# Convolution taps moved between an attention kernel's softmax steps and its first heads

## The reference

```python
h = _rmsnorm(x, g_pre_mix)
z = h @ w_in + b_in
q, k, v, cva, cvg = jnp.split(z, [D_ATTN, 2 * D_ATTN, 3 * D_ATTN, 3 * D_ATTN + D_CV], axis=-1)
attn = moba_fn(q, k, v)                       # 8 heads x 64, blocks of 256, best 3 blocks and the own one
glu = cva * jax.nn.sigmoid(cvg)
c = _causal_dwconv(jnp.concatenate([cv_hist, glu], axis=1), w_cv_dw, b_cv_dw)   # 31 taps, 512 channels
c = jax.nn.silu(_layernorm(c, g_cv_ln, b_cv_ln)) @ w_cv_pw + b_cv_pw
x = x + _rmsnorm(jnp.concatenate([attn, c], axis=-1) @ w_out, g_post_mix)
# then a gated feed-forward part with a convolution of three taps, 1024 -> 2 x 2816 -> 1024
```

## Time and profile before

| what | value |
|---|---|
| median of 3 runs | 1112.55 us (1112.46 to 1114.36) |
| the profiled execution | 1111.6 us |
| its span in the trace | 1109.8 us |
| mean granted clock of TensorE | 0.935 of 2.4 GHz |
| busy: PE, PEld | 956.3 us (86%), 702.5 us (63%) |
| busy: DVE, ACT, POOL | 697.8 us (63%), 446.0 us (40%), 460.2 us (41%) |
| moved by DMA | 205.19 MB, mean 185 GB/s |

### The profile page before, as it was taken

How to read it: one execution, slowest core, us unless ns; L and a number is a source line. 1 busy time by engine, 2 the same in 40 slices (tenths; PEclk the granted TensorE clock), 3 DMA queues, 4 the chain that set the end, 5 groups by cost and what they waited for, 6 DMA issues and landing times.

```text
span 1109.8 us, 19606 instructions
## 1 busy us (share of the span) xinstructions
PE 956.3 (86%) x7520; PEld 702.5 (63%) x7520; DVE 697.8 (63%) x920; ACT 446.0 (40%) x892; POOL 460.2 (41%) x408
## 2 busy tenths in 40 slices
PE   3987869798795088987989987999999999999995
PEld 3545655454453045544645567999999999667663
DVE  3688695867574047677442556888888889523215
ACT  3334454666666644435230223233333323234332
POOL 1014355656563943461000334654556555323430
PEclk9998988989898579989899998999999999999998
DMA  9896979998988337886958211223322231222222
GB/s 320 294 314 230 352 250 320 330 351 302 324 306 282 134 119 231 283 281 221 398 173 236 74 41 39 77 77 95 96 77 77 77 114 39 76 65 87 76 72 85
DMA packets 155207, 205.19 MB, mean 185 GB/s; under 512 B 10097, under 2 KB 75634, under 8 KB 155072
## 3 DMA queue, kind: packets, MB, share of 16 engines
q1 hardware_dynamic: 154619, 202.33, 54.8%
q10 hardware_dynamic: 495, 1.62, 0.5%
HBM read 198.59 MB, written 5.68 MB: 184 GB/s over the span
## 4 chain that ended last, share of the span: by engine, by line
PE 68%; DVE 9%; POOL 9%; ACT 6%; issue 4%; DMA 2%; SPq 2%; POOLq 0%; DVEq 0%; ACTq 0%
POOL conv L1822 7%; PE tp L880 7%; PE z L880 6%; PE sc L880 6%; PE z L740 5%; PE sc L530 5%; PE ob L590 4%; PE z L625 4%; PE ob L880 3%; PE sm L880 3%; PE tp L911 3%; PE ob L911 3%; PE z L911 2%; PE sc L706 2%; DVE kT L1422 2%
## 5 line engine op out<-in xcount | busy, mean ns | idle before, releaser
L1822 POOL TENSOR_TENSOR conv<-conv,prod 128x576 f32<-128x576 f32 x120 | 174.8, 1457 | 122.9 <-ACT prod L1095 107.8
L1422 DVE STREAM_TRANSPOSE kT<-kN 128x2048 f32<-128x2048 f32 x64 | 145.6, 2295 | 35.4 <-DMA kN<-in_cache_k 34.9
L1094 ACT ACTIVATE prod<-glu,consts 128x512 f32<-128x512 f32 x124 | 89.1, 718 | 54.0 <-POOL conv L1822 50.2
L1862 POOL TENSOR_TENSOR wulo<-wu,wuhi 128x2048 fp32r<-128x2048 f32 x22 | 102.4, 4656 | 13.1 <-ACT wuhi L1164 13.1
L1880 POOL TENSOR_TENSOR wdlo<-wd,wdhi 128x1024 fp32r<-128x1024 f32 x22 | 57.4, 2610 | 90.0 <-ACT wdhi L1353 90.0
L1729 DVE TENSOR_TENSOR fTlo<-fT,fThi 128x1152 fp32r<-128x1152 f32 x22 | 29.7, 1355 | 91.6 <-ACT fThi L1352 91.6
L625 PE MATMUL z<-hT,wz 128*128 128x512 f32 x192 | 85.4, 598 | 0.0
L530 PE MATMUL sc<-kT,qS 128*32 128x256 f32 x1024 | 68.1, 411 | 11.7 <-DVE kT L1422 10.8
L1029 ACT ACTIVATE S<-sc 128x512 f32<-128x512 f32 x32 | 35.3, 1102 | 105.2 <-PE sc L530 105.2
L1754 DVE TENSOR_TENSOR cvo<-cvo,sg 128x576 f32<-128x576 f32 x22 | 76.1, 3460 | 0.0
L590 PE MATMUL ob<-vN,pT 128*32 128x128 f32 x2048 | 71.0, 288 | 0.0
(11 more groups left out here) (313 smaller groups left out, 2563.8 us busy)
## 6 DMA issues: line engine op xcount, KB each, us to landing
kN<-in_cache_k SPq DMA_DIRECT2D x256, 256.0 KB, 4.6
vN<-in_cache_v SPq DMA_DIRECT2D x256, 256.0 KB, 4.0
wu<-in_w_up SPq DMA_DIRECT2D x44, 512.0 KB, 4.7
wd<-in_w_down SPq DMA_DIRECT2D x22, 512.0 KB, 3.6
wz<-in_w_in SPq DMA_DIRECT2D x20, 512.0 KB, 7.3
wo<-in_w_out SPq DMA_DIRECT2D x1, 4096.0 KB, 15.4
xA<-in_x_prompt SPq DMA_DIRECT2D x4, 512.0 KB, 11.6
wq<-in_w_in SPq DMA_DIRECT2D x1, 2048.0 KB, 17.5
```

The lines of the kernel that those rows point to most:

```text
L1094: act.activation(dst[:, 0:TP_], glu[:, i, j:j + TP_], ACT.Copy, scale=w_cv[:, i, j:j + 1])
L1422: dve.transpose(kT[:, u % 4, :, :].rearrange("p c (i k) -> p i c k", i=4), kN[:, c % 3, :, :].rearrange("p i (c k) -> p i c k", k=32)).the ...
L1822: ins = pool.tensor_tensor(conv[:, i, :], conv[:, i, :], prod[:, n % 2, :], ALU.add).then_inc(s["prod_used"], 1)
L1862: pool.tensor_tensor(wulo[f % 2][:, :, :], wu[f % 2][:, :, :, :].rearrange("p k u n -> p k (u n)"), wuhi[f % 2][:, :, :].bitcast(F32), ALU ...
```

## The change

- ScalarE's order: in steps 1 to 3 there are 24 taps in place of 25, two of them now ahead of the first copy of scores, ten in place of 14 between the last copy of scores and `exps`; `exps` goes ahead of the move of the last tile. In step 0 eight in place of nine stand there.
- TensorE: for b < 4, `scores(b+1, 2)` goes behind u = 2 and `scores(b+1, 3)` behind u = 3, each ahead of the work that `fill` puts there.
- Step 4: its taps, now 26, are spread: 5, 3 and 3 around the first three heads, then 2, 3, 2 and 8. GpSimd's queue follows: `normalize(0)`, `(1)` and `(2)` stand behind 5, 3 and 3 adds, `normalize(3)` behind all.
- The rows leave the end of step 3 and go in three parts around the first two heads of step 4, on TensorE and ScalarE. SP's stores go behind values 8b+5.
- Step 0 on VectorE: `norm_out(0)` and `row_sums(1)` go ahead of `glu_values(3)` and of two key transposes.

```diff
+        TAPS_FIRST, TAPS_HEADS = 98, (5, 3, 3)
+
+        def scores_at(b):
+
+            return (0, 2, 2, 3) if b < 4 else (0, 2, 3, 4)
...
                     load_k(8 * b + 12)
                 if b < 4:
                     load_wz(2 * b + 3)
-                if b == 4:
-                    sp.wait_ge(s["v2_home"], 4)
-                    sp.wait_ge(s["vs_put"], 1)
-                    sp.dma_start(rows("v_p"), vP[:, 0:4, :]).then_inc(s["stored_v"], 16)
-                    sp.dma_start(a["v_s"][0].rearrange("b t h d -> (b t) (h d)"), vP[0:TS, 4, :]).then_inc(s["stored_cv"], 16)
-                    sp.wait_ge(s["knat_put"], TT)
-                    sp.dma_start(rows("k_p"), kNat[:, :, :]).then_inc(s["stored_k"], 16)
-                    sp.dma_start(a["k_s"][0].rearrange("b t h d -> (b t) (h d)"), kNs[0:TS, :]).then_inc(s["stored_ks"], 16)
-                    sp.wait_ge(s["glun_put"], 2)
-                    sp.dma_start(a["cv_p"][0, 0], cvT[0][0:CW - 1, :]).then_inc(s["stored_cv"], 16)
-                    sp.dma_start(a["cv_s"][0][:, CW - 1 - NT:CW - 1, :], cvT[1][0:TS, :]).then_inc(s["stored_cv"], 16)
                 load_v(8 * b + 4)
                 if b < NB - 1:
                     for c in range(8 * b + 13, 8 * b + 16):
...
                 load_v(8 * b + 5)
+                if b == 4:
+                    sp.wait_ge(s["v2_home"], 4)
+                    sp.wait_ge(s["vs_put"], 1)
...
+                    sp.dma_start(a["cv_s"][0][:, CW - 1 - NT:CW - 1, :], cvT[1][0:TS, :]).then_inc(s["stored_cv"], 16)
                 load_v(8 * b + 6)
...
-            def rows_out():
-
-                pe.wait_ge(s["z2_put"], 8)
-                pe.wait_ge(s["ot_put"], 3)
-                for t in range(TT):
+            def rows_out(part):
+
+                if part == 0:
+                    pe.wait_ge(s["z2_put"], 12)
+                    pe.wait_ge(s["ot_put"], 4)
+                for t in ((0, 1), (2, 3), (4,))[part]:
                     if t >= 2:
                         pe.wait_ge(s["knat_put"], t - 1)
                     for hp in range(HP):
                         src = kP[:, hp, t * P:(t + 1) * P] if t < 4 else kTs[:, hp, :]
                         ins = pe.transpose(TB[t % 2][0:tok(t), hp * P:(hp + 1) * P], src, ident)
                     ins.then_inc(s["knat_done"], 1)
+                if part < 2:
+                    return
                 pe.wait_ge(s["glus_put"], 1)
...
-                pe.wait_ge(s["glun_put"], 2)
 
...
                 pe.wait_ge(s["pnorm"], 4 * h + 4)
                 if h == 0:
-                    pe.wait_ge(s["ot_put"], 4)
+                    pe.wait_ge(s["glun_put"], 2)
...
                         tile(x + (0, 2, 4, 7).index(u))
-                    if b == 3 and u == 7:
-                        rows_out()
                 if b - 1 in HEADS_AT and u == 0:
...
                             pe.wait_ge(s["mu_put"], 2)
+                        if b == 4:
+                            rows_out(0)
                         s_head(h)
+                        if b == 4:
+                            rows_out(1)
                     elif u == 1:
                         s_head(h + 1)
+                        if b == 4:
+                            rows_out(2)
...
                             own_scores(b + 1)
-                        if u in (0, 2, 3, 4):
-                            scores(b + 1, (0, 2, 3, 4).index(u))
+                        for j in range(4):
+                            if u == scores_at(b)[j]:
+                                scores(b + 1, j)
                     fill(b, u)
...
-            def put_rows():
-                act.wait_ge(s["z1_put"], 8)
-                act.wait_ge(s["z2_done"], 12)
-                act.activation(gluS[:, :, :].rearrange("p c (b t) -> p c b t", b=NB), gs[:, :, :, CW - 1:SX], ACT.Copy).then_inc(s["glus_put"], 1)
-                for t in range(TT):
+            def put_rows(part):
+                if part == 0:
+                    act.wait_ge(s["z1_put"], 8)
+                    act.wait_ge(s["z2_done"], 12)
+                    act.activation(gluS[:, :, :].rearrange("p c (b t) -> p c b t", b=NB), gs[:, :, :, CW - 1:SX], ACT.Copy).then_inc(s["glus_put"], 1)
+                for t in ((0, 1), (2, 3), (4,))[part]:
...
                 if b:
                     put_out(b - 1)
+                if b in TILES_AT:
+                    taps(2)
                 put_scores(b + 1, 0)
                 if b == 0:
                     taps(2)
                     gate_exp(2, 0)
                     taps(2)
                     gate_exp(2, 1)
+                    taps(1)
                     put_scores(1, 1)
+                    put_scores(1, 2)
                     taps(5)
-                    put_scores(1, 2)
                     put_scores(1, 3)
                     spread_q(2)
-                    taps(1)
+                    taps(2)
                     gate_exp(3, 0)
                     taps(2)
                     gate_exp(3, 1)
-                    taps(6)
+                    taps(4)
                     exps(1)
                 elif b in TILES_AT:
                     x = TILES_AT[b]
                     taps(5)
                     put_tile(x)
-                    taps(1)
+                    taps(2)
                     put_scores(b + 1, 1)
+                    put_scores(b + 1, 2)
                     taps(5)
                     put_tile(x + 1)
-                    put_scores(b + 1, 2)
                     if x < 8:
                         put_turned_value(x // 2)
                     put_scores(b + 1, 3)
                     spread_q(b + 2)
                     taps(4)
                     put_tile(x + 2)
-                    taps(3)
+                    taps(4)
                     if x < 8:
                         put_turned_value(x // 2 + 1)
-                    taps(5)
-                    put_tile(x + 3)
                     taps(2)
                     exps(b + 1)
-                    if b == 3:
-                        put_rows()
-                        put_tails()
+                    put_tile(x + 3)
                 elif b in HEADS_AT:
                     h = HEADS_AT[b]
                     if b == 4:
-                        taps(CT * CW)
+                        put_rows(0)
                     else:
                         p_turned(h - 1)
                     p_exps(h)
+                    if b == 4:
+                        put_rows(1)
+                        assert tap["n"] == TAPS_FIRST
+                        taps(TAPS_HEADS[0])
                     p_exps(h + 1)
                     if b == 5:
                         roots_of_variance()
+                    else:
+                        put_rows(2)
+                        put_tails()
+                        taps(TAPS_HEADS[1])
                     put_scores(b + 1, 1)
                     p_turned(h)
+                    if b == 4:
+                        taps(TAPS_HEADS[2])
                     put_scores(b + 1, 2)
                     p_exps(h + 2)
+                    if b == 4:
+                        taps(2)
                     put_scores(b + 1, 3)
-                    if b < 6:
-                        spread_q(b + 2)
+                    spread_q(b + 2)
                     p_turned(h + 1)
+                    if b == 4:
+                        taps(3)
                     p_exps(h + 3)
+                    if b == 4:
+                        taps(2)
                     p_turned(h + 2)
+                    if b == 4:
+                        taps(CT * CW)
                     exps(b + 1)
                     if b == 4:
                         mean()
...
                 if b == 0:
                     gate(3)
+                    norm_out(0)
+                    row_sums(1)
                     glu_values(3)
                 if b < NB - 2:
                     turn_k(b + 2, 0)
                     turn_k(b + 2, 1)
-                norm_out(b)
-                row_sums(b + 1)
+                if b:
+                    norm_out(b)
+                    row_sums(b + 1)
...
+            def sums(first, behind):
...
-            for h in range(4):
+            n = TAPS_FIRST
+            sums(0, n)
+            for h in range(3):
+                sums(n, n + TAPS_HEADS[h])
+                n += TAPS_HEADS[h]
                 normalize(h)
+            sums(n, CT * CW)
+            normalize(3)
             pool.wait_ge(s["mu_put"], 2)
```

More of the change, by code:

```diff
@@ L1814, in _ @@
             pool.wait_ge(s["c_loaded"], 16)
-            for n in range(CT * CW):
-                i, j = n // CW, n % CW
-                pool.wait_ge(s["prod_put"], n + 1)
-                if j == 0:
-                    pool.tensor_scalar(conv[:, i, :], prod[:, n % 2, :], w_cv[:, i, CW:CW + 1], None, ALU.add).then_inc(s["prod_used"], 1)
-                else:
-                    pool.wait_ge(s["prod_used"], n)
```

(16 more changed lines are left out.)

7 lines of the change are left out of this document (added).

## The result

The changed kernel took 1108.72 us (median of 15 runs, 1101.12 to 1119.79), the kernel before 1113.6 us (15 runs, 1107.65 to 1115.5): ratio 0.9943, 95% interval 0.9925 to 0.9961. The forecast was 1091 and its range ended at 1104.

A forecast was written before the change was run, and what follows sets the result against it. Steps 1 to 3 were taken as nearly full of loads, with ScalarE's softmax queued behind taps paced by GpSimd. Gains of 12.8 us up to W(4) and 7.6 in step 4, 20.4 together, took 1111.6 to 1091; range 1077 to 1104.

The forecast's parts named there:

- SP's queue: Steps 1 to 3: scores(b+1,2) ahead of weigh(b,3) delays SP's loads; cycle 59.6 us, so steps 1 and 2 gain nothing.
- rival 2: Steps 1 to 3: loads keep pace, a step falls to 52.4 us, total 1075; chance 0.14.
- `exps` to the end of `weigh(b,0)`: End of softmax's stretch, steps 1 to 3: 8.2 us, against 7.9 before, with the last tile's move now between.
- S + 12.7: S is SP's first value load of a step; the third score group's keys are transposed 12.7 us later.
- Half of the gain was the rows' block: End of step 3: half of the 12.8 us gained comes from the rows' block, moved and not removed.
- Step 4: the failed sum: Step 4 with spread taps and rows: 80.9 us to the channel sums' end, 88.5 before, a gain of 7.6 us.
- W(4): Mark at the end of weigh(4,0): forecast at 340.4 instead of 353.2, a gain of 12.8 us up to it.
- Behind step 4 nothing changes: After the channel sums: nothing found that changes but the start; loads of step 5 released as before.
- rival 6: Nothing changes: SP's cycle at 66 us eats both gains, total 1112; chance 0.03.
- Rival 3: Step 4 gives back what it gets: heads and taps delay each other, 88.5 us stays, total 1099; chance 0.20.
- Rival 4: Step 4: two-input VectorE instructions hold GpSimd's adds, sums end some 5 us later, total 1096; chance 0.10.
- Rival 5: Step 4: slow stores delay p_turned(0); the sum turns if they land after +49; 1118 at +55; chance 0.07.

The follow-up runs named there:

- again: The changed kernel once more, unedited: 1110.38 us (1095.91 to 1115.71), ratio 0.9955; its profiled execution 1110.56 us.
- Experiments 2 to 5: Changed kernel with third and fourth score groups back, 1085.0 us; key loads issued earlier, 1095.32; only third group back, 1089.22; kernel before with early groups alone, 1115.79.
- experiment 3: Changed kernel with SP issuing three key chunks ahead of value chunk 8b+7 in steps 0 to 3, no compute instruction moved: 1095.32 us, ratio 0.9847.
- scores_old: Changed kernel with the third and fourth score groups of steps 0 to 3, and ScalarE's copy of the third, back in their old places: 1085.0 us, ratio 0.9760.
- Experiment 6: Rows back at step 3's end, SP's stores at step 4's front: on the changed kernel 1106.8 us, on scores_old 1084.41 us.
- even_after: Changed kernel with step 4's taps dealt otherwise: three ahead of the first scores' copy, six behind p_turned(0), four behind p_exps(3): 1091.3 us, ratio 0.9807.
- taps_front: Changed kernel with all 26 taps of step 4 in one row ahead of the first head: 1124.37 us, ratio 1.0098.
- taps_even: scores_old with step 4's taps dealt otherwise: three ahead of the first scores' copy, six behind p_turned(0), four behind p_exps(3): 1072.38 us, ratio 0.9641.
- taps_rank: scores_old with three taps of step 4 moved from behind p_turned(1) to behind p_turned(0): 1084.23 us, ratio 0.9748.

## Why the forecast was wrong, by its own steps

**SP's queue: right in mechanism, in size nearly.** The forecast said that the third score group ahead of `weigh(b,3)` would hold SP, TensorE would stand idle ahead of that group, and the step would be 59.6 us, 58.1 and 1.5 for the clock. Measured: 61.2 and 59.3, and 62.6 and 60.4 in `again`. TensorE stood idle there for 8.2, 3.2 and 3.5 us, where some 6 were forecast. Experiments 2 to 5 show it from four sides, with the reserve under experiment 3. What the forecast did not do is price the moved groups by themselves: inside this change they are a loss of 24 us. The steps of 54 us that `scores_old` shows (first value loads at 164.76, 219.35 and 273.34) stood under rival 2, as a matter of the load rate, where they were a matter of SP's queue.

**`exps` to the end of `weigh(b,0)`: 8.2 forecast, 10.1 to 12.3 measured.** I had VectorE's penalties end 18.0 and ScalarE's taps 18.5 us behind the copy, "so ScalarE stays last, just". The second half of `exps(2)` waits 2.09 us for VectorE, and `weigh(2,0)` ends at 225.9, 12.3 us behind 213.63. In steps 1 and 2 SP's queue hides that. Ahead of step 4 nothing hides it: `exps(4)` started at 333.25 (332.2 forecast), and from there to 343.35 are 10.1 us, with `weigh(4,0)` at 1.94 instead of 1.11 us and the transposes at the lower clock as well. These 1.9 us and the 1.05 by which `exps(4)` came late are the difference between 12.8 and 9.8 us in the first execution. In `again` the same 10.1 us follow an `exps(4)` at 339.67, as the loads of steps 1 to 3 came later; there the gain is 3.4. Of the 9.4 us missing then, 2.1 lie ahead of step 1's first value load (171.34, 169.2 forecast), 3.8 in steps 1 and 2, 1.2 in step 3's keys (third group at S + 13.9 instead of S + 12.7), 0.4 between it and `exps(4)`, and 1.9 behind `exps(4)`.

**Half of the gain was the rows' block: no gain at all.** That term was said to be "moved and not removed", and step 4 was costed with it. Experiment 6 agrees with this: 5.4 us out, 5.7 us in.

**Step 4: the failed sum.** Forecast 80.9 us from W(4) to the sums' end; measured 90.0 and 86.6. The front in the first execution: the own scores wait for VectorE behind a late key chunk, the row transposes start at +5.2 instead of +2.1, `p_exps(0)` ends at +13.8 instead of +10.1, and this delay stays, in `p_turned(0)` at +32.9 (28.6 forecast). In `scores_old`, with the keys on time, these are +9.7 and +29.3: that part was forecast well. The heads from there to `p_exps(3)`'s end took 32.8 us in place of 29.3, and 32.7 in `scores_old`; there the forecast copied the old chain's length, and the matmuls of it ran at a lower clock. The sums took 7.07 in place of 6.05. In `again` the 5.7 us too many are 1.4 in front of `p_turned(0)`, 3.4 in the heads, 0.4 in the adds and 0.5 in the sums. What was forecast rightly is what the ten serial adds cost, and what was not asked is why they should stand there: GpSimd was idle for 7.87 and 4.95 us among the heads, and `even_after` fills that.

**"Behind step 4 nothing changes": wrong.** In `again` and in the six other executions with sums of 6.6 us, 672.4 us lie behind them in place of 668.1: 4.3 us. The rows put it at the clock of 0.61 from 15.5 to 28.7 us behind the sums; the forecast had the clock fall inside the sums only.

**Sum for the execution nearest the median, `again`:** a gain of 3.4 up to W(4) and 1.9 in step 4, less 4.3 behind it: 1109.8 - 1.0 = 1108.8. Of the forecast's 20.4 us, 9.4 were lost ahead of W(4) (7.5 with the loads up to `exps(4)`, 1.9 behind `exps(4)`), 5.7 in step 4 (3.4 of it in the heads), 4.3 behind it. In the first changed execution the loads cost only 1.05 of these 7.5 us, and the full clock behind the sums gave 2.2 us; that it lies 8 us under the median is luck of that execution.

**The rivals.** In the number rival 6 (nothing changes, 1112) came nearest, but not by its mechanism: SP's cycle was 59.3 to 62.6 us and not 66. Rival 3 (step 4 keeps its 88.5 us, 1099) had step 4's length about right, with 90.0 and 86.6, but that the taps and heads only delay each other is not so: `taps_front` and `even_after` show that placing the taps is worth 14 us and more. Rival 2's short steps are real, at 54.0 and 54.6 us for its 52.4, with the groups in their old places. Rival 4: the adds stayed at 16.06 / 10 = 1.61 us at the end and 4.50 / 3 = 1.50 us beside the ranking in `scores_old`, while VectorE's pair went from 0.76 to 3.12 us. The Trainium skill ("SBUF — State Buffer", Who interferes with whom) has both sides blocked fully; the trace agrees for VectorE and shows no held GpSimd. Rival 5: the stores landed 1.94 us after ScalarE was ready, nothing near +49.

**Open:** why single executions of one kernel differ by up to 20 us (15 in the kernel before), and what decides which of two clock courses an execution takes behind the sums.

## What to carry to other kernels

When an edit moves a waiting instruction ahead of one that frees a buffer, read the queue that waits for that buffer: here a score group that waited 3 to 8 us for its keys ahead of `weigh(b,3)` kept SP waiting for 28.5 us in all, and one line, with the copy that goes with it, cost 24 us where the softmax was short and 5 where it wasn't. A forecast that finds such a coupling should price that part of the change alone. And work dealt into gaps should leave none at the end of the row: six serial adds, 9.2 us, cost 11.5 us up to the sums' end. Some 5 us of clock came on top behind them in seven of the nine executions that had them.

## What the runs showed of the hardware

- TensorE's clock can fall well behind a pause, while TensorE is busy. After 9.69 us idle and 16 matmuls in 6.62 us (clock 0.62 in them), it ran at 1.00 for 15.5 us, of which it was busy for 13.9 (`scores_old`), and then at 0.61 for 13.2 us, busy throughout; the work of that stretch took 4.6 us more, the sums 2.5 us more. Seven executions show this course, with 9.6 to 9.7 us idle. It did not come after 0.4 us idle (`taps_even`, `even_after`), nor in two others with a pause: 9.26 us and sums of 7.07 us at 0.58 (first changed execution), and 11.03 us and sums of 6.04 us (`taps_rank`, clock 0.68).
- Two of VectorE's two-input instructions of 256 columns took 3.12 us beside GpSimd's adds and 0.76 without; an add took 4.50 / 3 = 1.50 us beside them and 7.59 / 5 = 1.52 us without.
